# A two-layer decoder step on one Trainium2 core: decayed keys turned by DVE and DMA, F and Q sums behind the gate, last pair's products and page scores in another order

## The reference

```python
def step(s, inp):
    qc, kc, vc, gc = inp
    cum = jnp.cumsum(gc, axis=2)
    o_inter = jnp.einsum('bhtk,bhkv->bhtv', qc * jnp.exp(cum), s)
    ...
    o = o_inter + jnp.einsum('bhts,bhsv->bhtv', att, vc)
    last = cum[:, :, -1:, :]
    s_new = jnp.exp(last[:, :, 0, :])[..., None] * s + jnp.einsum(
        'bhsk,bhsv->bhkv', kc * jnp.exp(last - cum), vc)
    return s_new, o
...
proj = rms_norm(x, norm_g) @ w_in
...
def fox_layer(x, norm_g, w_in, q_norm, w_o, k_all, v_all, c_all):
    bsz, t, _ = x.shape
    q, gate = jnp.split(rms_norm(x, norm_g) @ w_in, 2, axis=-1)
    ...
    o = forgetting_attention(q, k_all, v_all, c_all)
    o = o.reshape(bsz, t, B_WIDTH).astype(x.dtype) * jax.nn.silu(gate)
    return x + o @ w_o
```

## Time and profile before

| | |
|---|---|
| median of 3 runs | 1507.69 us (1505.27 to 1508.44) |
| the profiled execution | 1507.58 us |
| its span, first to last instruction | 1505.9 us |
| PE busy | 1475.1 us, 98% of the span |
| DVE, ACT, POOL busy | 1000.4, 670.3, 415.6 us |
| PE's longest wait | 10.4 us in 2 waits at the start (L2139) |
| mean DMA rate | 205 GB/s |

### The profile page before, as it was taken

How to read it: one execution, slowest core, us unless ns; L and a number is a source line. 1 busy time by engine, 2 the same in 40 slices (tenths; PEclk the granted TensorE clock), 3 DMA queues, 4 the chain that set the end, 5 groups by cost and what they waited for, 6 DMA issues and landing times.

```text
span 1505.9 us, 24074 instructions
## 1 busy us (share of the span) xinstructions
PE 1475.1 (98%) x8757; PEld 1082.5 (72%) x8757; DVE 1000.4 (66%) x1995; ACT 670.3 (45%) x1364; POOL 415.6 (28%) x335
## 2 busy tenths in 40 slices
PE   7999999999999999999999999999999999998998
PEld 6788888888888875446777777777777777764443
DVE  6878696978878694126377676768777676756421
ACT  4435545444435552212356555545555555555100
POOL 5012312121212101012051525344442615422200
PEclk9999999999999999999999999999999999999999
DMA  9975757767675744323246869696978879598731
GB/s 273 289 222 155 226 170 211 225 201 230 199 215 155 226 149 138 102 65 128 61 118 198 260 200 309 184 273 203 287 232 233 277 223 297 175 361 302 251 127 58
DMA packets 296267, 308.96 MB, mean 205 GB/s; under 512 B 26502, under 2 KB 252030, under 8 KB 296150
## 3 DMA queue, kind: packets, MB, share of 16 engines
q1 hardware_dynamic: 285014, 270.84, 59.1%
q0 software_dynamic: 11136, 36.59, 7.0%
HBM read 247.76 MB, written 126.73 MB: 249 GB/s over the span
## 4 chain that ended last, share of the span: by engine, by line
PE 88%; DVE 5%; ACT 4%; issue 2%; DMA 1%; POOL 0%; SPq 0%; DVEq 0%; POOLq 0%
PE psum L2187 45%; PE psum L2211 7%; PE psum L2701 7%; PE psum L2498 5%; PE psum L2524 4%; PE psum L2264 3%; PE psum L2150 2%; PE psum L2458 2%; PE psum L2556 2%; ACT psum L1307 1%; PE psum L2346 1%; PE psum L2330 1%; PE psum L2275 1%; PE psum L2350 1%; ACT psum L1316 1%
## 5 line engine op out<-in xcount | busy, mean ns | idle before, releaser
L2187 PE MATMUL psum<-arena 128*128 128x252 f32 (+1 forms) x3472 | 812.0, 385 | 2.2 <-DVE arena L1484 2.2
L2187 PEld LDWEIGHTS psum<-arena 128*128 128x128 f32 x3472 | 640.8, 190 | 125.2 <-issue 24.3
L985 POOL TENSOR_TENSOR arena<-arena 128x1024 f32<-128x1024 f32 x64 | 156.7, 2448 | 378.1 <-DMA arena<-k_pages 372.4
L1484 DVE TENSOR_TENSOR arena<-arena,psum 128x252 f32<-128x252 f32 (+1 forms) x310 | 129.0, 416 | 146.8 <-PE psum L2187 142.0
L2701 PE MATMUL psum<-arena 128*128 128x512 f32 x256 | 115.7, 604 | 0.2 <-DVE arena L1911 0.2
L2211 PE MATMUL psum<-arena 128*128 128x512 f32 x256 | 113.0, 594 | 0.1
L1060 ACT COPY arena<-psum 128x252 f32<-128x252 f32 (+1 forms) x124 | 46.3, 373 | 139.7 <-PE psum L2187 139.6
L2701 PEld LDWEIGHTS psum<-arena 128*128 128x128 f32 x256 | 47.7, 192 | 58.9 <-issue 57.8
L1123 ACT ACTIVATE arena<-arena 128x1024 f32<-128x1024 f32 x48 | 50.6, 1054 | 85.7 <-DVE arena L1530 85.5
L2211 PEld LDWEIGHTS psum<-arena 128*128 128x128 f32 x256 | 47.5, 190 | 57.4 <-issue 56.5
L1307 ACT ACTIVATE psum<-psum,arena 128x640 f32<-128x640 f32 (+3 forms) x64 | 59.0, 921 | 63.0 <-DVE arena L1844 63.0
(11 more groups left out here) (270 smaller groups left out, 2046.1 us busy)
## 6 DMA issues: line engine op xcount, KB each, us to landing
k_pages<-in_cache_k SPq DMA_DIRECT2D x64, 512.0 KB, 6.4
v_pages<-in_cache_v SPq DMA_DIRECT2D x64, 512.0 KB, 7.0
arena<-k_pages SPq DMA_DIRECT2D x64, 512.0 KB, 5.2
arena<-v_pages SPq DMA_DIRECT2D x64, 512.0 KB, 6.4
arena<-in_w_in_a SPq DMA_DIRECT2D x32, 512.0 KB, 7.2
arena<-in_x_prompt SPq DMA_DIRECT2D x16, 512.0 KB, 7.4
arena<-in_w_kv SPq DMA_DIRECT2D x16, 512.0 KB, 6.3
arena<-in_w_in_b SPq DMA_DIRECT2D x16, 512.0 KB, 7.4
```

The source lines that it names most:

```text
L985: pool.tensor_tensor(k_ring[:, m % 2], k_ring[:, m % 2], q_all[:, m % S:m % S + 1, :].broadcast_to([P, PAGES, P]), ALU.mult).then_inc(kq_m ...
L1484: dve.tensor_tensor(out, more, bank[n % 2][:, 0:size(u)], ALU.add).then_inc(of.by_dve, 1)
L2187: ins = pe.matmul(bank[n % 2][:, 0:size(u)], w[:, k, :], x[:, k, :], start=(k == 0 and r in (0, 1, 3, 4)), stop=(k == HK - 1), skip_group_ ...
```

## The change

There are four parts. (1) The decayed keys go the way of V: DVE turns them in 32 x 32 blocks, SP stores and loads them (a second set of `token_rows`), and the 8 transposes on PE and the 2 PSUM copies on ACT are gone. What is loaded has the key dimension in four groups of 32, so an update is four products with 32 output partitions each. The updates stand behind `fq(8, 9)` in heads 0 to 6. The keys' exponentials and k_dec are made earlier, and k_dec has another buffer. (2) POOL makes the F and Q sums for the head after the next at the end of a head, behind DVE's gate step `sg`, not at the start of the next. (3) In the last head the updates stay ahead of an output part, and the loads of the residual `res_in` go behind the token copies on SP. (4) In the last pair four products of the output projection stand ahead of `scores(p, 5)`, of which one stood ahead of it and three behind it, and the page scores `score(m)` to `score(m + 2)` come later on DVE.

```diff
-TOKEN_SETS = 1
+TOKEN_SETS = 2
...
-        k_dec = logf[:, 0:T]
+        k_dec = t1[:, 0:T]
...
-        k_dec_tok = o_rs[:, 0:T].rearrange("p (t k) -> p t k", k=P)
+        k_blocks = o_rs[:, 0:T]
+        k_dec_tok = k_blocks.rearrange("p (g t l) -> p t g l", g=4, l=32)
...
             def tokens_in(h, n, blocks):
-                sp.wait_ge(rows_stored, STORES * token_set(h, n))
+                sp.wait_ge(rows_stored, STORES * token_set(h, TOKEN_SETS - 1 if h == AH - 1 else n))
...
-                    res_in(0)
-                    res_in(1)
-                    tokens_out(h, 0, v_blocks)
-                tokens_in(h, 0, v_blocks)
-                if h < AH - 1:
+                    tokens_out(h, 0, v_blocks)
+                if h < AH - 1:
+                    tokens_in(h, 0, v_blocks)
+                    tokens_out(h, 1, k_blocks)
+                else:
+                    tokens_out(h, 1, k_blocks)
+                    tokens_in(h, 0, v_blocks)
+                tokens_in(h, 1, k_blocks)
+                if h + 1 == AH:
+                    res_in(0)
+                    res_in(1)
+                else:
                     sort_pages(sp, h + 1, 1)
...
             def head(h):
                 pool.dma_start(s_smp, state_in[h]).then_inc(state_loaded, 16)
-                if h + 1 < AH:
-                    if h:
-                        pool.wait_ge(units.done, fq_unit(h, 14))
-                    w_sums(h + 1, F, Q, sums_fq, fq_sums)
+                if h == 0:
+                    w_sums(1, F, Q, sums_fq, fq_sums)
...
                 pool.dma_start(prompt_out[h], s_all[:, NC - 1, :]).then_inc(prompt_stored, 16)
+                if h + 2 < AH:
+                    pool.wait_ge(units.done, fq_unit(h + 1, 11))
+                    pool.wait_ge(vecs.sem, vecs.at("sg", h))
+                    w_sums(h + 2, F, Q, sums_fq, fq_sums, last_free=(units.done, fq_unit(h + 1, 13)))
...
                 level(8)
+                for t in range(NC):
+                    end = t * P if t >= NC // 2 else t * P + C - 1
+                    ins = act.activation(t1[:, cols(t)], cum[:, cols(t)], ACT.Exp, bias=cum[:, end:end + 1], scale=-1.0)
+                ins.then_inc(acts.sem, 1)
                 level(4)
...
                 fq(2)
-                for t in range(NC):
-                    end = t * P if t >= NC // 2 else t * P + C - 1
-                    ins = act.activation(t1[:, cols(t)], cum[:, cols(t)], ACT.Exp, bias=cum[:, end:end + 1], scale=-1.0)
-                ins.then_inc(acts.sem, 1)
...
-                for j in range(2):
-                    act.wait_ge(uu_done.sem, uu_done.at(f"turn{j}", h))
-                    act.copy(k_dec_tok[:, 4 * j:4 * j + 4, :], bank[4 + j][:, :]).then_inc(uu_taken_a, 1)
...
                 merge(4)
+                a("exp_kd")
+                dve.tensor_tensor(k_dec, k_h[:, 0:T], t1[:, 0:T], ALU.mult).then_inc(vecs.sem, 1)
+                dve.wait_ge(vecs.sem, vecs.at("k_dec", h))
+                turn_tokens(1, k_blocks, k_dec)
                 a("s_kept")
...
                 dve.wait_ge(s_all_free, h + 1)
+                fq(8)
                 chunk_states(0)
-                fq(8)
...
-                score(m)
+                if nxt:
+                    score(m)
                 row_max(p, 4)
...
                 turn_blocks(p, 4, 0, 1)
-                score(m + 1)
+                score(m + 1 if nxt else m)
...
                 kq(11)
-                score(m + 2)
+                if nxt:
+                    score(m + 2)
...
                 turn_blocks(p, 5, 0, 1)
+                if not nxt:
+                    score(m + 1)
...
                 vg(1)
+                if not nxt:
+                    score(m + 2)
                 score(m + 3)
...
-                v("k_dec")
-                for j in range(2):
-                    pe.wait_ge(uu_taken_v, 4 * h + 5 + j)
-                    for t in range(4 * j, 4 * j + 4):
-                        ins = pe.transpose(bank[4 + j][:, t % 4 * P:(t % 4 + 1) * P], k_dec[:, cols(t)], ident)
-                    ins.then_inc(uu_done.sem, 1)
...
                 fq(7)
-                pe.wait_ge(pt_moved, MOVES * token_set(h, 0))
-                pe.wait_ge(uu_taken_a, 2 * h + 2)
-                for j in range(2):
-                    for c in range(4 * j, 4 * j + 4):
-                        ins = pe.matmul(bank[4 + j][:, c % 4 * P:(c % 4 + 1) * P], k_dec_tok[:, block_of(c), :], v_tok[:, block_of(c)],
-                                        start=True, stop=True)
-                    ins.then_inc(uu_done.sem, 1)
                 pe.wait_ge(acts.sem, acts.at("sq_smp", h))
...
-                fq(8, 9, 10)
+                if h + 1 < AH:
+                    fq(8, 9)
+                pe.wait_ge(pt_moved, MOVES * token_set(h, 1))
+                for j in range(2):
+                    pe.wait_ge(uu_taken_v, 4 * h + 5 + j)
+                    for c in range(4 * j, 4 * j + 4):
+                        for g in range(4):
+                            ins = pe.matmul(bank[4 + j][32 * g:32 * g + 32, c % 4 * P:(c % 4 + 1) * P], k_dec_tok[:, block_of(c), g],
+                                            v_tok[:, block_of(c)], start=True, stop=True, skip_group_check=True)
+                    ins.then_inc(uu_done.sem, 1)
+                if h + 1 == AH:
+                    fq(8, 9)
+                fq(10)
...
                 new_score(p)
                 kq_n(8, 9)
-                last((1, 4, 5))
+                last((1, 4, 7), (0, 6, 7))
                 scores(p, 5)
                 kq_n(10, 11)
-                last((1, 5, 7), (0, 6, 7))
                 if p:
                     decode(p - 1, 1)
```

More of the change, by code:

```diff
@@ L387, in build @@
         smp_done = Marks(sem("smp_done"), "k_smp", "v_smp", "o_row", "o_smp", "mean_smp")
-        uu_done = Marks(sem("uu_done"), "outer0", "outer1", "turn0", "turn1", "upd0", "upd1")
+        uu_done = Marks(sem("uu_done"), "outer0", "outer1", "upd0", "upd1")
         ob_done = Marks(sem("ob_done"), "o0", "o1")
         lv_taken_v, lv_taken_a = sem("lv_taken_v"), sem("lv_taken_a")
-        uu_taken_v, uu_taken_a = sem("uu_taken_v"), sem("uu_taken_a")
-        acts = Marks(sem("acts"), "ln_f", "ln_q", "sig_q", "exp64", "k", "decays", "exp32", "exp_cum", "exp16", "exp8", "exp4", "exp2",
-                     "s_kept", "exp1", "exp_kd", "ln_g", "sq_smp", "ln_smp", "sig_g")
+        uu_taken_v = sem("uu_taken_v")
+        acts = Marks(sem("acts"), "ln_f", "ln_q", "sig_q", "exp64", "k", "decays", "exp32", "exp_cum", "exp16", "exp8", "exp_kd", "exp4", "exp2",
+                     "s_kept", "exp1", "ln_g", "sq_smp", "ln_smp", "sig_g")
         vecs = Marks(sem("vecs"), "logf", "cum", "q_in", "diff64", "k_in", "q", "fact64", "diff32",
                      "fact32", "diff16", "fact16", "diff8", "k_smp", "fact8", "diff4", "fact4", "diff2", "v_diag", "fact2",
-                     "fact1", "k_dec", "o_row", "g_in", "o_smp", "q_dec", "sg")
+                     "k_dec", "fact1", "o_row", "g_in", "o_smp", "q_dec", "sg")
         o_strips_set, o_strips_stored, o_rs_loaded = sem("o_strips_set"), sem("o_strips_stored"), sem("o_rs_loaded")
@@ L845, in _, with block_sums @@
             me = Steps(pool, w_steps)
-            def block_sums(one, two, out, done):
+            def block_sums(one, two, out, done, last_free=None):
                 me.did(pool.tensor_tensor(out[:, 0], two[:, 0:HK], two[:, HK:KT], ALU.add))
@@ L851, in block_sums, with w_sums @@
                 me.chain(pool.tensor_tensor(out[:, 1], out[:, 0], one[:, 0:HK], ALU.subtract))
+                if last_free:
+                    pool.wait_ge(*last_free)
                 pool.tensor_tensor(out[:, 2], one[:, HK:KT], out[:, 1], ALU.subtract).then_inc(done, 1)
-            def w_sums(h, y1, y2, out, done):
+            def w_sums(h, y1, y2, out, done, last_free=None):
                 par = h % 2
                 pool.wait_ge(w_a_loaded[par], w_a_in(h))
-                block_sums(w_a[:, par, :, y1, :], w_a[:, par, :, y2, :], out, done)
+                block_sums(w_a[:, par, :, y1, :], w_a[:, par, :, y2, :], out, done, last_free)
             def sums_of_kq(q):
@@ L1663, in head @@
                 fq(4)
-                a("exp_kd")
-                dve.tensor_tensor(k_dec, k_h[:, 0:T], t1[:, 0:T], ALU.mult).then_inc(vecs.sem, 1)
                 merge(1)
```

## The result

The changed kernel takes 1512.32 us (median of 12 runs) against 1507.81 before: the ratio is 1.0034 (95% interval 1.0027 to 1.0042), slower by 4.5 us and by more than 0.2%. The prediction was 1501.5, range 1497 to 1506. The profiled execution has a span of 1509.9 us, 4.0 more than before.

A forecast was written before the change was run, and what follows sets the result against it. PE, busy 1475.1 of 1505.9 us, was taken to bound the kernel. From 1507.58 us, 4.8 came off for layer A (5.2 − 0.4) and 1.3 for the last pair: 1501.5, range 1497 to 1506.

The forecast's parts named there:

- the last one on layer A: Head 7: token loads wait for both sets of stores but no longer for the residual; priced 0, bounds 1 either way.
- Removed 0.90 and added 0.16: PE's work per head: transposes gone saves 0.90 us, narrow updates add 0.16; net 0.74, or 5.2 in heads 0 to 6.
- the narrow block: Updates as 64 narrow instructions on PE: 0.09 us more than the wide form plus 0.07 for one step, 0.16 a head.
- The tokens in heads 0 to 6: PE's updates wait for the second copy through DRAM: 0.4 us of stall in all, 0.5 late in head 2.
- the 1.4 that I took without a row for it: Layer A: time the four stores of k_dec take behind V's load before the second load is issued, 1.4 us.
- Level 1: Layer A: PE's wait for DVE's factor, delayed 1.2 us with 1.2 to spare; taken as 0, at most 1.2 a head.
- The F and Q sums: POOL's sums in layer A need only be there a head later and PE waited for none; price 0.
- The last pair: Last pair: 1.6 us gained up to scores(6), less 0.3 for the moved page scores; 1.3 us in sum.
- 4.7 − 3.1 = 1.6: Last pair: scores(6) comes 4.7 us earlier, less 3.1 lost to the clock falling again; 1.6 left.
- 0.3 was forecast: Last pair: page scores coming later on DVE delay the last scores by at most 0.5 us; 0.3 taken.
- The clock term: Last pair: one new wait of 2.4 us lets PE's clock fall again, a loss of 3.1 us.
- my second case: Last pair: all as forecast, but the clock stays up; 3.1 us less, 1498.4 us; chance 0.25.

The follow-up runs named there:

- e2: The kernel before, with the last head's two residual loads moved behind V's token copy on SP: 1512.62 us, ratio 1.0032.
- e1: The changed kernel with both residual loads put back ahead of the token copies on SP in the last head: 1509.25 us, ratio 1.0011.
- e3: The changed kernel with only the first of the two residual loads ahead of the token copies in the last head: 1506.79 us, ratio 0.9998.
- e5: The changed kernel, last head back to PE transposes, wide updates and one token copy, one residual load ahead of it, one behind: 1501.0 us, ratio 0.9963.
- e10: The kernel before, with the updates of all 8 heads as 32 products of 32 output partitions, in place: 1509.68 us, ratio 1.0018.
- e6: As e5, with the updates of heads 0 to 6 one unit later on PE, behind fq(10): 1503.92 us, ratio 0.9978.
- e4: The changed kernel with the last pair as in the kernel before: 1512.37 us, ratio 1.0039.
- e8: The changed kernel with POOL making the F and Q sums at the start of the next head again: 1518.43 us, ratio 1.0078.

## Why the prediction was wrong, step by step

**The step that failed** is the last one on layer A: "In head 7 both loads wait for both sets of stores, while the residual's 1 MB no longer queues ahead of them: these two answer each other; I take 0, bounds 1 either way." It counted what the moved loads do for the token copies and did not ask who waits for the residual itself. DVE's addition does, and PE's turns stand behind DVE. For the tokens alone the two did about answer each other: their loads were issued at 567.27, 4.5 us earlier than V's before (571.74), while PE came 4.0 us earlier. The term should have read +9.2: e2 shows the wait alone in the old kernel (+5.9 by the medians, with one token copy ahead of the residual instead of two), e1 and e3 remove it and pay 5.6 and 5.1 for the token copies instead, and e5 takes the whole change out of the last head.

e5 lands at 1501.0, near the 1501.5 that the other steps add up to, but this is luck in part: from the first head's outer products to the last head's it gains 3.0 us where 4.8 was forecast, and in the last pair 2.9 where 1.3 was.

**Heads 0 to 6.** Removed 0.90 and added 0.16, so 0.74 a head, was the forecast; a head without a wait gained 0.57. The mis-sized term is the narrow block, 0.34 by the trace and 0.30 to 0.34 by e10: I counted the step into the narrow tiles once, at 0.07, and not the step out of them. The drain that the Trainium skill names for a change of tiling mode (TensorEngine Tiling (Array Packing), Key Properties) agrees in sign with e10's rows, 0.10 at either end.

**The tokens in heads 0 to 6** were priced well: a stall of 0.4 in all was forecast and 0.6 measured, in one head (not head 2, where the row of before was the latest). In head 4 V's load landed at 360.15 + 6.8 = 367.0 and the second load was issued at 369.70, so the stores took 2.7 and not the 1.4 that I took without a row for it, but V's load took 1.0 less than before. The second load landed 3.6 us after its issue (3.2 forecast). In the other kernels the waits at the updates of these heads came to between nothing (e6) and 2.3 us in all (e4).

**What I priced at nothing.** Level 1 waits for nothing, as forecast. The F and Q sums cost nothing here, but for another reason than I gave: I held that PE waits for none of them, without asking what their old place does once the updates come later. Without the move the change would have cost some 6 us more (e8).

**The last pair** gained 1.4 where 1.3 was forecast, with the wait of 2.46 at `decode` (2.4 forecast). The agreement in the sum is luck, as two of its terms were off: `scores(6)` comes 3.1 us earlier, counted from block 4, where 4.7 − 3.1 = 1.6 was forecast, since the half clock cost 1.6 and not 3.1 (3.40 in place of 1.93, and 5.57 in place of 5.42 for the products behind); and block 7 gives 1.7 back where 0.3 was forecast. The clock term was wrong in reasoning too. In e1 and e3 the same wait of 2.46 was followed by no half clock (the 64 products behind it take 1.93, and the granted clock of e1 is 1.00 from 1375.80 to 1384.00), in the changed kernel, e5, e6 and e8 by some (3.40, 3.16, 2.50 and 2.68). Yet the pair took 34.9 and 35.0 us in e1 and e3 and 34.2 to 35.7 in the others: at the scores of block 7 PE waits for DVE's turned block, 1.58 in the changed kernel, 1.89 in e1 and e3, 0.31 in e5 and 0.21 in e6. So my second case, 3.1 us better with the full clock, did not come true where the clock was full: e1 and e3 were 0.8 and 0.7 us better than the changed kernel there.

**The rivals.** The result is on the slower side, to which I gave 0.08 for a token load of 5.5 us or more in heads 0 to 6. That is not what happened. The slower side came about for a reason that stood in no rival.

## What to carry to other kernels

When a load is moved behind others on a queue, look first at its own consumer and at what queues behind that consumer; the gain for what it made way for comes second. A step that pays in a loop can lose in the last turn, where the queue holds other loads: price the last turn by itself, and leave it in the old form if it doesn't pay. (No run tried the last head's updates two units later, behind the output part, as they stand in the other heads.) An edit that costs nothing where it stands can still be needed by another edit of the same change, so test it inside the changed kernel and alone.

## What the runs showed of the hardware

A step from 128-wide tiles into 32-wide ones or back cost 0.10 us each at these products (e10). Behind the same idle time of 2.46 us on PE the granted clock stayed at 1.00 in e1 and e3 and was 0.50 for a stretch in the changed kernel, e5, e6 and e8; behind idle times of 3.00 (e3) and 4.83 us (e1) it was 0.50, and a block of 1.95 us took 3.64 and 3.41. A DVE operation of 1.23 us took 3.26 beside two POOL operations of 1.28 and 1.27 us (e8).
